# A three-block fp32 transformer kernel on one core: the first block's mixer run in two passes, tokens 0 to 127 first, with expert rows gathered beside the second pass

## The chip, the cores and the metric

The kernel runs on one core of one Trainium2 chip. The metric is device time in microseconds (us) of one execution; lower is better. A core has five engines, each with its own instruction stream: TensorE (PE), VectorE (DVE), ScalarE (ACT), GpSimd (POOL) and SyncE (SP), which here only issues DMAs. They meet through semaphores.

## The reference, cut to what matters

Three blocks run one after the other on 512 tokens of 1024 features, all in fp32. Only the first is changed. It is a mixer (retention and spatial gating) and then a layer that picks, for each token, 128 of 16384 experts:

```python
mod = silu(c) @ w_ada + b_ada                 # six rows: shift, scale, gate, twice
h = modulate(rms_norm(x, norm1_g), shift1, scale1)
q, k, v, g_ret, u, sv, gate_a, gate_b = split(h @ w_in)        # 1024 -> 7168
y_ret = head_norm(retention(rotary(q), rotary(k), v), ret_gn_g) # causal over all 512 tokens
branch_a = (silu(g_ret) * y_ret) @ w_ret_out
branch_b = spatial_gating(gelu(u), gelu(sv), ...) @ w_sgu_out   # mixes within 128 tokens
x = x + gate1 * ((sigmoid(gate_a) * branch_a + sigmoid(gate_b) * branch_b) @ w_out)
h2 = modulate(rms_norm(x, norm2_g), shift2, scale2)
s = einsum(h2 @ w_q, sub_keys)                # 8 heads, two halves, 128 keys each
expert, g = top 16 of the 16 x 16 sums of the two halves' top 16, softmax   # 128 picks a token
act = gelu(einsum('td,thkd->thk', h2, expert_u[expert])) * g
x = x + gate2 * einsum('thk,thkd->td', act, expert_v[expert])
```

A token needs only itself and earlier tokens of the mixer, so tokens 0 to 127 can go through the whole mixer before the others.

## The kernel before, in words

Tokens stand in 4 tiles of 128 partitions. A projection is cut into chunks of 512 output columns, a chunk into two pieces (halves of the 1024 inputs) of 1 MB. `load_ahead` (L94) has SP load the pieces into `ring_raw` in an order fixed by `plan_one` (L1924). `split_piece` (L135) has DVE make two rounded parts of each piece, `ring_high` (a cast, L130) and `ring_low` (a subtraction, L132). PE then takes three fast products in place of one plain fp32 product (`product`, L174, lines L176 to L178). A matmul of plain fp32 operands has two records in the trace, each with its weight load; one of the split parts has one.

The first block (`block_one`, L1917) is a row of stages with a barrier between them:

- `first_rows` (L929) is the entry: the first two of the six `mod` rows are summed on DVE from eight 1 MB lines of `w_ada` (`add_lines`, L920, recorded as L923), the input is normed, transposed on PE and split into `h_features`.
- `first_mixer` (L1339) runs 20 chunks for all 4 tiles, in ten calls of `project`, `project_along` and `closing`. The last 16 lines of `w_ada` are added beside the first chunks. Rotary, retention, norms and gating are interleaved with the projections by hand-made tables (L1064 to L1066). `closing` (L720) adds to `x`, norms each tile and transposes it (L770).
- `peer` (L1492) computes the queries of all tokens (16 query blocks, pieces of `peer_w_q`), scores them against the keys (`score_unit`, L1580), and `route` has DVE find the top 16 and the expert numbers. One unit is 2 heads, 32 picks of each of 128 tokens; a tile has 4 units. For pick n of a tile POOL gathers one row per token (L1566): 128 rows of 8 KB, u and v side by side, 1 MB. DVE takes the product of u with `h` (`dot`, L1756) and PE adds the v half into PSUM with two plain fp32 matmuls by a scaled diagonal (L1655), which DVE makes (`weigh`, L1749). There are 4 x 128 = 512 picks. The first 10 are gathered during the query stage and summed on DVE instead (`sum_early`, L1769); the rest follow at the speed of the gathers, through 12 slots of SBUF.
- `leave` (L1427) closes the block.

What sets the order around the change: each engine's stream is in program order; SP issues a piece when its slot is free; POOL gathers into a slot when its former pick has been used (`used_slot` or `taken_early`).

Of the kernel before, what the change touches and what calls it, by code (L numbers as in the profile page):

```python
# [23 lines left out]
P = 128  # L24
SEQ = 512
NT = SEQ // P
D = 1024
# [50 lines left out]
def over(nc, under, name, shape, dtype=F32):  # L78

    return nc.alloc_sbuf_tensor_at(f"{name}_{next(NUMBERS)}", shape, dtype, offset=PLACES[under.name])  # L80
# [828 lines left out]
SGU_GROUPS, SGU_DIM = 4, 256  # L909

# [14 lines left out]

WARMING = 4


def first_rows(nc, core, d, mod, c_col, gain):  # L929
# [5 lines left out]
    plan_splits(core, 1)  # L935
    with stage(nc, "entry", "zeroed", "c_loaded", "bias_loaded", "gain_loaded", "silu_done", "used", "multiplied", "summed", "shift_ready",
# [6 lines left out]
        def _(sp):  # L943
# [6 lines left out]
            load_ahead(core, sp, core.splits + 2)  # L950
# [12 lines left out]
        def _(act):  # L963
# [14 lines left out]
            copy_transposed(nc, core, act, KD, core.hT[0], transposed, copied)  # L978
# [16 lines left out]
        def _(dve):  # L995
# [9 lines left out]
            def lower(t):  # L1005
                for n in (2 * t, 2 * t + 1):
                    at = transposed_bank(KD, n)
                    dve.wait_ge(copied, n + 1)
                    nc.vector.tensor_tensor(core.hT[1][at], transposed_view(core, n), core.hT[0][at].bitcast(F32), ALU.subtract)
# [12 lines left out]
            split_piece(nc, core, dve, 0, 0)  # L1022
# [7 lines left out]
            for t in range(NT):  # L1030
# [4 lines left out]
                if t == 2:  # L1035
                    lower(0)
# [3 lines left out]


def other_rows(nc, core, d, mod, c_col):

    ring = over(nc, core.h, "ada_ring", [P, 2, ADA_LINE])
    lines = [(part, k) for k in range(KD) for part in (1, 2)]
    signals = ("ada_used", "ada_landed0", "ada_landed1")

    def pool_part(pool, used, *landed):
        for n, (part, k) in enumerate(lines):
            if n >= 2:  # L1050
                pool.wait_ge(used, n - 1)
            pool.dma_start(ring[:, n % 2, :], ada_lines(d, part, k)).then_inc(landed[n % 2], 16)

    def dve_part(dve, used, *landed):
        for n, (part, k) in enumerate(lines):
            dve.wait_ge(landed[n % 2], 16 * (n // 2 + 1))
            rows = mod[:, 2 * part:2 * part + 2, :].rearrange("p a f -> p (a f)")
            add_lines(nc, dve, rows, ring[:, n % 2, :], c_col[:, k:k + 1]).then_inc(used, 1)
            yield

    return signals, pool_part, dve_part, None, None


# [5 lines left out]
def retention(nc, core, d, mod, qk, v, rot, qkT, y, cosine, sine):  # L1069
# [13 lines left out]
    def pe_part(pe, loaded, rotated, transposed, moved, spread, cleared, decay_loaded, scored, weighted, summed, copied):  # L1083
        def spread_rows(n):
            for q in (2 * n, 2 * n + 1):
                if q >= 4:
                    pe.wait_ge(cleared, q - 3)
                nc.tensor.matmul(core.ps[:, q % 4, :], core.ones[:], rows[:, q * BANK:(q + 1) * BANK], start=True, stop=True).then_inc(spread, 1)

        def turn(t):  # L1090
            pe.wait_ge(rotated, t + 1)
            if t:
                pe.wait_ge(moved, 2 * t)
# [3102 lines left out]
```

## Time and profile before

| | us |
|---|---|
| median of 3 runs | 4110.15 (4108.12 to 4110.21) |
| the profiled execution, its span from first to last instruction | 4104.9 |
| entry | 0 to 55.9 |
| mixer of the first block, all 4 tiles | 55.9 to 583.9 |
| query stage, with 20 gathers issued | 583.9 to 690 |
| gathering stage of the first block | 690 to about 1956 |
| second and third block | the rest |

No time of the profiled execution other than its span is given; the median of the runs is 5.25 us above that span, for what lies around it. Over the span PE is busy 87%, DVE 69%, POOL 22%, ACT 20%. In the page's slices the DMA engines are busy 9 tenths or more from about 720 to 1950 us, and 2 to 6 tenths in the mixer. Busy shares of PE there are of modelled ends: a record lasts longer than the distance to the next one, so the pace of PE is read from the distance between starts.

### The profile page before, as it was taken

To read this page: it belongs to the slowest core of one execution; us is meant where nothing else is said; L and a number is where in the kernel's file an instruction comes from. 1 tells how busy PE (TensorE), PEld (TensorE's weight loads), DVE (VectorE), ACT (ScalarE), POOL (GpSimd) and SP (SyncE) were. 2 spreads that over 40 slices of the span, in tenths; PEclk is the share of its full clock that TensorE was granted. 3 is DMA by queue.
4 is the path that set the end of the run, shared out by engine and by line. 5 is a ranking of instruction groups with operands and counts; after the bars stand their busy time and mean duration, and the time that the engine had idled before them with its cause. 6 is when DMAs were issued, how large, how long until landed. Compare 5 with 4: busy or idle time off the path is not lost. (4 is left out here: it accounts for less than half of the span.)

```text
span 4104.9 us, 43525 instructions
## 1 busy us (share of the span) xinstructions
PE 3577.6 (87%) x15786; PEld 2429.3 (59%) x15786; DVE 2847.4 (69%) x5103; ACT 836.9 (20%) x1657; POOL 903.5 (22%) x852
## 2 busy tenths in 40 slices
PE   7999988878778777777899997967978999999998
PEld 5778876223223222222667776856756787877876
DVE  7653668878878877865755567666867558757775
ACT  1110112111111111110121135316842212411000
POOL 2010003434444444443000111214630000100000
PEclk9999999999999999999999998988988999999999
DMA  6522227999999999998334522119953233222221
GB/s 252 176 83 93 96 103 302 419 423 423 423 423 424 423 420 416 412 418 357 119 120 136 171 83 102 58 65 399 421 226 93 65 106 97 84 95 94 99 87 70
DMA packets 206417, 910.60 MB, mean 222 GB/s; under 512 B 20830, under 2 KB 25838, under 8 KB 126738
## 3 DMA queue, kind: packets, MB, share of 16 engines
q0 software_dynamic: 93040, 665.54, 39.7%
q1 hardware_dynamic: 108272, 233.47, 17.0%
q10 hardware_dynamic: 4900, 8.94, 0.6%
q8 instruction: 119, 1.95, 0.2%
q14 instruction: 86, 0.70, 0.0%
HBM read 878.97 MB, written 40.97 MB: 224 GB/s over the span
## 5 line engine op out<-in xcount | busy, mean ns | idle before, releaser
L130 DVE CAST ring_high<-ring_raw 128x2048 fp32r<-128x2048 f32 (+2 forms) x166 | 192.4, 1159 | 426.9 <-PE psum L178 348.1
L176 PE MATMUL psum<-ring_high,h_features 128*128 128x512 f32 x1128 | 459.3, 407 | 23.9 <-PEq L48 16.0
L178 PE MATMUL psum<-ring_high,h_features 128*128 128x512 f32 x1128 | 446.3, 396 | 0.0
L177 PE MATMUL psum<-ring_low,h_features 128*128 128x512 f32 x1128 | 445.8, 395 | 0.0
L1655 PE MATMUL psum<-slots_ring,evacuation_tmp 128*128 128x512 f32 x672 | 334.2, 620 | 92.6 <-DVE evacuation_tmp L1749 92.6
L132 DVE TENSOR_TENSOR ring_low<-ring_raw,ring_high 128x2048 fp32r<-128x2048 f32 (+2 forms) x166 | 358.1, 2157 | 12.8 <-issue 0.4
L176 PE MATMUL psum<-h_features,ring_high 128*128 128x512 f32 (+3 forms) x888 | 350.7, 395 | 14.0 <-DVEq L287 5.5
L177 PE MATMUL psum<-h_features,ring_high 128*128 128x512 f32 (+3 forms) x888 | 347.2, 391 | 0.0
L178 PE MATMUL psum<-h_features,ring_low 128*128 128x512 f32 (+3 forms) x888 | 346.7, 390 | 0.0
L1871 ACT ACTIVATE weight<-score 128x1 f32<-128x1 f32 x512 | 103.6, 203 | 1124.8 <-DVE score L1756 1124.6
L1655 PE MATMUL psum<-slots_features,evacuation_tmp 128*128 128x512 f32 x504 | 250.1, 620 | 64.3 <-DVE evacuation_tmp L1749 64.2
L1655 PEld LDWEIGHTS psum<-slots_ring,evacuation_tmp 128*128 128x128 f32 x672 | 114.7, 190 | 311.3 <-DVE evacuation_tmp L1749 227.9
L176 PEld LDWEIGHTS psum<-ring_high,h_features 128*128 128x128 f32 x1128 | 216.5, 192 | 73.7 <-issue 15.9
L1756 DVE CUSTOM_DVE_ANT_0 slots_ring<-slots_ring,h_tokens 128x1024 f32<-128x1024 f32 x168 | 205.5, 1223 | 76.4 <-DMA slots_ring<-in_peer_uv,expert 73.5
L178 PEld LDWEIGHTS psum<-ring_high,h_features 128*128 128x128 f32 x1128 | 215.5, 191 | 47.1
L177 PEld LDWEIGHTS psum<-ring_low,h_features 128*128 128x128 f32 x1128 | 216.6, 192 | 42.5 <-issue 0.5
L1566 POOL DMA_INDIRECT slots_ring<-in_peer_uv,expert x168 | 175.9, 1047 | 252.0 <-PE psum L1655 235.1
L1655 PEld LDWEIGHTS psum<-slots_features,evacuation_tmp 128*128 128x128 f32 x504 | 86.4, 190 | 227.2 <-DVE evacuation_tmp L1749 164.5
L645 POOL TENSOR_SCALAR mean_var<-mean_var 128x1 f32<-128x1 f32 (+3 forms) x25 | 11.3, 452 | 941.8 <-DVEq L3961 378.1
L1655 PE MATMUL psum<-slots_raw,evacuation_tmp 128*128 128x512 f32 x332 | 165.7, 622 | 46.9 <-DVE evacuation_tmp L1749 46.9
L1655 PE MATMUL psum<-slots_mod,evacuation_tmp 128*128 128x512 f32 x336 | 165.7, 617 | 41.5 <-DVE evacuation_tmp L1749 41.4
L176 PEld LDWEIGHTS psum<-h_features,ring_high 128*128 128x128 f32 (+2 forms) x888 | 166.0, 187 | 53.7 <-issue 10.1
(667 smaller groups left out, 7003.9 us busy)
## 6 DMA issues: line engine op xcount, KB each, us to landing
ring_raw<-in_w_in SPq DMA_DIRECT2D x94, 1024.0 KB, 5.3
ring_raw<-in_w_up_pairs SPq DMA_DIRECT2D x20, 1024.0 KB, 5.0
ada_ring<-in_w_ada POOLq DMA_DIRECT2D x16, 1024.0 KB, 5.5
ring_raw<-in_w_out SPq DMA_DIRECT2D x12, 1024.0 KB, 5.0
moe_entries<-in_const_zero_rows POOLq DMA_DIRECT2D x23, 512.0 KB, 5.0
row_room<-moe_entries SPq DMA_DIRECT2D x23, 512.0 KB, 11.0
moe_results<-rows_out SPq DMA_DIRECT2D x23, 512.0 KB, 7.6
ring_raw<-in_w_down SPq DMA_DIRECT2D x10, 1024.0 KB, 4.8
```

Of the source, the lines that this page charges most:

```text
L130: nc.vector.tensor_copy(high, whole)
L132: return nc.vector.tensor_tensor(low, whole, high.bitcast(F32), ALU.subtract)
L176: nc.tensor.matmul(out, a[0], b[0], start=start, stop=False)
L177: nc.tensor.matmul(out, a[0], b[1], start=False, stop=False)
L178: return nc.tensor.matmul(out, a[1], b[0], start=False, stop=stop)
L645: nc.gpsimd.tensor_scalar(v, v, eps, None, ALU.add).then_inc(done, 1)
L1566: nc.gpsimd.indirect_dma_start(out=slots[slot_of[n]], out_offset=None, in_=rows, in_offset=bass.IndirectOffsetOnAxis(ap=expert[:, t, i:i + ...
L1655: mm = nc.tensor.matmul(banks(t)[q], diagonal[:, n % DIAGONALS, :], slots[slot_of[n]][:, D + q * BANK:D + (q + 1) * BANK], start=i == (0 i ...
L1756: nc.vector.tensor_tensor_reduce(out=u, in0=u, in1=core.h[:, t, :], scale=1.0, scalar=0.0, op0=ALU.mult, op1=ALU.add, accum_out=score[:, i ...
L1871: nc.scalar.activation(weight[:, i:i + 1], score[:, i:i + 1], ACT.Gelu).then_inc(activated, 1)
```

## The change

The mixer of the first block becomes one stage that runs 20 chunks twice. The first pass takes tile 0 alone, with plain fp32 matmuls whose moving operand is the piece as loaded, so nothing is split (`mixer_pe`, the branch `p.native`). It ends with the four query chunks, the scores and the routing of tile 0. The second pass takes tiles 1 to 3 with split pieces, loaded again; the cast is now ACT's and the subtraction DVE's. Beside it, DVE routes units 1 to 3 of tile 0 and takes the dot products of 57 picks, ACT scales their v rows (`scale_picks`), and POOL adds them up (`add_pick`), through 5 slots. The query stage then holds only tiles 1 to 3, with 20 more picks taken the same way, and the gathers that are left (the PE sum starts at pick 77) go through 13 slots. Retention in the second pass takes tile 0's keys and values from what the first pass kept.

```diff
-EARLY = 10
-SLOTS_UV = 12
+EARLY_PICKS = 57
+POOL_PICKS = 77
+SLOTS_UV = 13
...
+ALONE_SLOTS = [n % WIDE_SLOTS for n in range(40)] + [4, 5, 0, 2, 6, 7, 1, 3]
...
+def mixer_pe(nc, core, pe, p):
+    for q, (c, half) in enumerate(p.pieces[0:2 * MIX_CHUNKS]):
+        for i in range(n):
+            pace.until(due(p.at["pe"], n * q + i))
...
+                if p.native:
+                    mm = nc.tensor.matmul(bank(c, i), x[0], w[0], start=kk == 0, stop=kk == KD - 1)
+                else:
+                    mm = product(nc, bank(c, i), x, w, kk == 0, kk == KD - 1)
...
+def scale_picks(nc, act, k, lo, hi):
+    act.wait_ge(k.dotted, hi)
+    nc.scalar.activation(k.weight[:, lo:hi], k.score[:, lo:hi], ACT.Gelu).then_inc(k.activated, hi - lo)
...
+        nc.scalar.activation(v, v, ACT.Copy, scale=k.weight[:, n:n + 1]).then_inc(k.scaled, 1)
...
+def add_pick(nc, core, pool, k, n):
...
+        pool.wait_ge(k.taken, n)
+        nc.gpsimd.tensor_tensor(total, total, v, ALU.add).then_inc(k.taken, 1)
...
+        one = Pass(sems[0:len(PASS_SIGNALS)], (0,), True, ALONE_PIECES)
+        two = Pass(sems[len(PASS_SIGNALS):2 * len(PASS_SIGNALS)], (1, 2, 3), False, REST_PIECES)
...
+            mixer_pe(nc, core, pe, one)
+            for j in range(UNITS):
+                query(j)
+                if j:
+                    score_unit(j - 1)
+            mixer_pe(nc, core, pe, two)
...
+            for n in range(EARLY_PICKS):
+                q = due(REST_DOTS, n)
+                pace.until(due(two.at["pool"], q + 1))
+                add_pick(nc, core, pool, k, n)
+                gather_until(n)
```

Where side work stands is set by tables of step numbers; two lines of them, each number the piece (for PE the piece and tile) before which a step is taken:

```diff
+           "dve": [4, 4, 5, 8, 9, 10, 11, 12, 13, 13, 14, 14, 15, 15, 23, 24, 24, 24, 25, 26, 28, 28, 29, 30, 31, 31, 35, 35, 35, 36, 36, 36],
+REST_ROUTE = [7, 15, 23, 26, 26, 28, 35, 42, 47, 52, 57, 62, 62, 62, 65, 69, 76, 78]
```

On PE, the mixer began with three split products for each quarter of a piece (before):

```order
L176 MATMUL psum<-ring_high,h_features 128x512
L177 MATMUL psum<-ring_low,h_features 128x512
L178 MATMUL psum<-ring_high,h_features 128x512
L176 MATMUL psum<-ring_high,h_features 128x512
L177 MATMUL psum<-ring_low,h_features 128x512
```

The same place after, from the last chunk of the first pass over the start of the queries (`wide_` are pieces as loaded, `alone_cT` and `h_alone` are tile 0's features):

```order
L1038 MATMUL psum<-wide_80,alone_cT_337 128x512 x4
L1038 MATMUL psum<-wide_81,alone_cT_337 128x512 x4
L1062 MATMUL psum<-ident,h_tokens 128x128 x8
L1938 MATMUL psum<-h_alone_77,wide_82 128x128 x4
L1938 MATMUL psum<-h_alone_77,wide_83 128x128 x4
```

A piece of the first pass is 4 matmuls where it was 48, and the 8 transposes of the closed tile stand directly between the last chunk and the queries.

On DVE, where the retained heads are normed, before (`gate_a` stage):

```order
L627 BN_STATS bn_parts<-a 128x6 x16
L630 BN_AGGR mean_var<-bn_parts 128x2 x16
L1249 SCALAR_TENSOR_TENSOR mod<-mod,row_b 128x1024
L1254 TENSOR_SCALAR a<-a,mean_var 128x256 x4
L1257 TENSOR_TENSOR a<-a,x_tokens 128x1024
L130 CAST ring_high<-ring_raw 128x2048
L132 TENSOR_TENSOR ring_low<-ring_raw,ring_high 128x2048
```

The same place in the second pass (L1703 is the dot product of a pick, L1226 the subtraction for one piece):

```order
L1226 TENSOR_TENSOR rest_raw_low_340<-wide_79,ring_high 128x2048
L1342 TENSOR_SCALAR a<-a,mean_var 128x256 x4
L1345 TENSOR_TENSOR a<-a,x_tokens 128x1024
L1342 TENSOR_SCALAR a<-a,mean_var 128x256 x4
L1345 TENSOR_TENSOR a<-a,x_tokens 128x1024
L1703 ISA slots_first_75,score<-slots_first_75,h_tokens 128x1024
L1703 ISA score 128x1
L1226 TENSOR_TENSOR ring_low<-wide_82,ring_low 128x2048
L1703 ISA slots_mod_74,score<-slots_mod_74,h_tokens 128x1024
L1703 ISA score 128x1
```

The casts have left DVE, and dot products and routing steps now stand between the splits.

On POOL, the mixer before held DMA issues and a few small operations; in the second pass it reads so (`fifth`, `slots_first` and `slots_mod` are slots of gathered rows, `x_tokens` the running sum):

```order
L1731 TENSOR_TENSOR x_tokens<-x_tokens,fifth 128x1024
L1692 DMA fifth<-in_peer_uv,expert 128x2048
L1731 TENSOR_TENSOR x_tokens<-x_tokens,slots_first_75 128x1024
L1692 DMA slots_first_75<-in_peer_uv,expert 128x2048
L1731 TENSOR_TENSOR x_tokens<-x_tokens,slots_mod_74 128x1024
L1692 DMA slots_mod_74<-in_peer_uv,expert 128x2048
```

Each gather stands behind the addition that frees its slot; there are 76 such additions of 128 x 1024 and one copy.

## Rows read from the trace of the kernel before

**Rows 1.** Busy time of each engine by stretch: mixer, query stage, gathering stage.
```profile
core 0: us, PE busy (x) PEld busy (x) DVE busy (x) ACT busy (x) POOL busy (x), PEclk, DMA share, GB/s
55.90:583.90 528.00, 505.12 (x2240) 410.07 (x2240) 304.53 (x323) 70.24 (x116) 34.79 (x35) 0.98 0.35 121
586.00:690.00 104.00, 98.33 (x476) 84.18 (x476) 74.46 (x174) 33.04 (x48) 27.72 (x21) 0.97 0.61 226
690.00:1936.00 1246.00, 985.22 (x2039) 344.69 (x2040) 986.70 (x2444) 143.40 (x545) 529.45 (x505) 0.99 1.01 419
```

**Rows 2.** Timeline, POOL then PE, gathering stage: start us, us, engine, line, operation.
```profile
689.92 1.07 POOL L1566 DMA_INDIRECT slots_mod<-in_peer_uv,expert  x1 [0.30 <-issue]
...
899.51 0.98 POOL L1566 DMA_INDIRECT slots_rows<-in_peer_uv,expert  x1 [1.51 <-PE psum L1655]
...
1952.04 3.70 PE L1655 MATMUL psum<-slots_mod,evacuation_tmp 128*128 128x512 f32 x8 [0.44 <-DVE evacuation_tmp L1749]
```

**Rows 3.** Timeline of PE: split products, score matmuls; weight loads of plain fp32.
```profile
71.22 0.39 PE L177 MATMUL psum<-ring_low,h_features 128*128 128x512 f32 x1
71.45 0.39 PE L178 MATMUL psum<-ring_high,h_features 128*128 128x512 f32 x1
...
597.01 1.05 PE L1580 MATMUL psum<-keysT,qT 128*128 128x128 f32 x8
598.95 0.33 PE L176 MATMUL psum<-h_features,ring_high 128*128 128x384 f32 x1
599.12 0.33 PE L177 MATMUL psum<-h_features,ring_high 128*128 128x384 f32 x1
...
22.74 0.19 PEld L986 LDWEIGHTS psum<-x_tokens,ones 128*128 128x128 f32 x1 [0.24 <-issue]
```

**Rows 4.** Groups by line and shape, DVE: from 0 to 700 us; last, gathering stage.
```profile
L132 DVE TENSOR_TENSOR ring_low<-ring_raw,ring_high 128x2048 fp32r<-128x2048 f32 x40 | 91.7, 2292 | 3.3 <-issue 0.4
L923 DVE SCALAR_TENSOR_TENSOR mod<-ada_ring,c_col,mod 128x2048 f32<-128x2048 f32 x23 | 54.1, 2352 | 25.6 <-DMA ada_ring<-in_w_ada 15.7 <-DMA mod<-in_b_ada 8.8
L130 DVE CAST ring_high<-ring_raw 128x2048 fp32r<-128x2048 f32 x40 | 49.0, 1225 | 141.7 <-PE psum L178 121.7 <-PEq L48 20.0
L1756 DVE CUSTOM_DVE_ANT_0 slots_mod<-slots_mod,h_tokens 128x1024 f32<-128x1024 f32 x6 | 7.2, 1222 | 3.1 <-DMA slots_mod<-in_peer_uv,expert 3.1
...
L1749 DVE TENSOR_SCALAR evacuation_tmp<-ident,weight,gates 128x128 f32<-128x128 f32 x494 | 169.4, 343 | 0.0
```

**Rows 5.** DVE and POOL at once: a group, then timelines of 246 and 2549 us.
```profile
L1238 POOL TENSOR_TENSOR x_tokens<-x_tokens,row_a 128x1024 f32<-128x1024 f32 x2 | 4.8, 2392 | 64.7 <-DMA row_b<-in_norm_g 64.7
...
246.01 5.52 DVE L1254 TENSOR_SCALAR a<-a,mean_var 128x256 f32<-128x256 f32 x4 [3.19 <-POOL mean_var L647]
256.25 1.38 DVE L1254 TENSOR_SCALAR a<-a,mean_var 128x256 f32<-128x256 f32 x4
...
2548.67 2.27 DVE L165 TENSOR_TENSOR ring_low<-ring_raw,ring_high 128x2048 fp32r<-128x2048 f32 x1
2550.86 1.28 DVE L2529 TENSOR_TENSOR keys<-hgrn_drop,k 128x256 f32<-128x256 f32 x1
2552.07 0.41 DVE L2530 TENSOR_TENSOR queries<-hgrn_drop,q 128x256 f32<-128x256 f32 x1
...
2548.84 3.02 POOL L2495 TENSOR_TENSOR hgrn_drop<-logs 128x512 f32<-128x512 f32 x1
```

**Rows 6.** Group by line and shape, ACT, the entry's scaled copy.
```profile
L974 ACT ACTIVATE h_tokens<-x_tokens,mean_var 128x1024 f32<-128x1024 f32 x4 | 4.6, 1148 | 22.3 <-POOL mean_var L960 22.3
```

**Rows 7.** Timeline of PE where the mixer closes: the last tiles' transposes.
```profile
571.27 1.04 PE L770 MATMUL psum<-ident,h_tokens 128*128 128x128 f32 x8
581.92 1.97 PE L770 MATMUL psum<-ident,h_tokens 128*128 128x128 f32 x8 [6.10 <-DVE h_tokens L860]
```

**Rows 8.** Timeline of the query stage: the first gather on POOL, its dot on DVE.
```profile
623.28 1.12 POOL L1566 DMA_INDIRECT slots_mod<-in_peer_uv,expert  x1 [35.09 <-DVE expert L1732]
...
629.00 1.23 DVE L1756 CUSTOM_DVE_ANT_0 slots_mod<-slots_mod,h_tokens 128x1024 f32<-128x1024 f32 x1 [1.12 <-DMA slots_mod<-in_peer_uv,expert]
```

More of the change, by code:

```diff
@@ L10 @@
 from contextlib import ExitStack, contextmanager
-from itertools import count
+from itertools import chain, count
 import numpy as np
@@ L1039, in _ @@
             lower(3)
[L1042 to L1061, printed above, removed]
@@ new lines, with raise_scores, start_gather @@
+TO_SHIFTED, ROUTE_STEPS = 17, 26
+def raise_scores(nc, act, k, m):
+    t, j = divmod(m, UNITS)
+    top = k.gates[:, t % 2, UNIT_HEADS * j:UNIT_HEADS * (j + 1), :]
+    act.wait_ge(k.shifted, m + 1)
+    nc.scalar.activation(top, top, ACT.Exp).then_inc(k.raised, 1)
+def start_gather(nc, pool, k, rows, n):
+    t, i = divmod(n, PICKS)
+    nc.gpsimd.indirect_dma_start(
+        out=k.slots[k.slot_of[n]], out_offset=None, in_=rows,
+        in_offset=bass.IndirectOffsetOnAxis(ap=k.expert[:, t, i:i + 1], axis=0),
+    ).then_inc(k.arrived[k.slot_of[n]], 16)
@@ new lines, in gather @@
+                def gather(n):
+                    slot, before = k.slot_of[n], k.last_of[n]
+                    if n % Q == 0:
+                        pool.wait_ge(k.routed, n // Q + 1)
+                    if before is None:
+                        if slot in (5, 6):
+                            pool.wait_ge(core.split[slot - 5], first + UNITS)
+                        elif slot in (7, 8):
+                            pool.wait_ge(core.used, first + UNITS)
+                        else:
+                            pool.wait_ge(projected, 1)
+                    elif before < POOL_PICKS:
+                        pool.wait_ge(k.taken, before + 1)
+                    else:
+                        pool.wait_ge(used_slot, before - POOL_PICKS + 1)
+                    start_gather(nc, pool, k, rows, n)
@@ L1570, in _ @@
+                for n in range(EARLY_PICKS, POOL_PICKS):
+                    add_pick(nc, core, pool, k, n)
+                    while k.issued < POOL_PICKS + 5 and k.last_of[k.issued] is not None and k.last_of[k.issued] <= n:
+                        gather(k.issued)
+                        k.issued += 1
+                for n in range(k.issued, TOTAL_PICKS):
+                    t, i = divmod(n, PICKS)
+                    gather(n)
                     if t and i == ROOT_PICKS[0]:
@@ L1843, in _ @@
                         weigh(n - 1)
-                    advance(router, 2 if n < EARLY + 6 else 1)
+                    advance(router, 1)
+                    if n % Q == Q - 1:
+                        for _ in router:
+                            pass
                     if t and i == 4:
@@ L1943 @@
+def plan_one(d):
+    return [("peer_q", cut) for cut in query_chunks(d)]
 STRIP = [0, 512, 896, 1152]
```

1554 lines of the change are left out of this document (968 added, 586 removed).

## The prediction

> **What bounds the kernel now.** I read the stages first: the windows by stretch [rows 1] cut the first block into mixer (528.0 us), query stage (583.9 to 690, 106 us) and gathering (1246 us of it). In the mixer PE is busy 505.1 of 528.0, DVE 304.5, and the DMA engines 35%: PE sets the pace and memory is idle. In the gathering stage the DMA share is 1.01 at 419 GB/s, and PE and DVE are at 79% each: the gathers set the pace. The timeline of that stage [rows 2] agrees: POOL's issues are 0.98 + 1.51 = 2.49 us apart and each waits for PE to release a slot that DMA filled. One pick is 1.049 MB, which at 419 GB/s is 2.50 us. So 128 rows gathered beside the mixer are worth 2.50 us each, if mixer work hides them.
>
> **Gathers, the gain.** At 690 us 20 gathers have been issued (POOL's 21 instructions in that window less one iota [rows 1]); the last matmuls end at 1952.04 + 3.70 = 1955.7 us [rows 2], 492 picks later. After the change POOL issues pick n when pick n-5 has been added, up to pick 81, and the eight new slots at once: 90 are out when the query stage ends. 70 fewer remain: 70 x 2.50 = **-175 us**. This is the whole gain; everything else is what it costs.
>
> **Mixer, PE's own work.** Split products of 512 columns start 0.2267 us apart (71.22 and 71.45, rounded), those of 384 columns 0.174 [rows 3]. A weight load of a plain fp32 matmul of 512 columns takes 0.19 after an idle 0.24, two loads to a matmul: 0.43 a record and 0.858 a matmul. Eight records of 128 columns take 1.05 with a tail of about 0.28: 0.11 a record, 0.22 for a score matmul [rows 3]; 0.43 and 0.64 for 256 and 384 columns follow by length.
> - Before: 1920 x 0.2267 = 435.3; 20 sets of 8 transposes x 0.88 = 17.6; retention scores 8.6, their products 17.2, spatial mixing 6.9, spreading `mod` 6.9: 492.5. The stage took 528.0, so 35.5 went in waits and in stretches at the lower clock.
> - First pass: 160 x 0.858 = 137.3, where this tile's share was 108.8; 5 sets of transposes, one tile's retention and mixing, the spreading 15.6: 152.9. Queries 128 x 0.22 = 28.2 and 16 score matmuls 3.5: 31.7.
> - Second pass: 1440 x 0.2267 = 326.4; transposes 13.2, scores 7.7, products 36 x 0.43 = 15.5, mixing 5.2: 368.0.
>
> Sum 552.6, which is 60.1 more than before.
>
> **Mixer, what is lost around it.** Memory in the first pass: 34 pieces, 13 `w_ada` lines and some 3.5 MB of constants, about 53 MB, at 419 GB/s [rows 1] 126 us against 153 of PE, with six pieces ahead. It is covered; if that cover went, each missing us would be PE's. With one tile there is no other tile's work over a chain, so I take 12 for waits inside the pass (bounds 0 and 35). Its close is bare: evacuation, statistics, two small POOL steps, gain, shift, transpose, copy. The mixer's last tile before shows PE waiting 6.10 for such a chain, and its 8 transposes then taking 1.97 instead of 1.04 [rows 7]; before they start and until the queries follow I take 12 (bounds 6 and 20). Start of the second pass, whose first splits are behind 12 routing steps on DVE: 5. Its own close over three tiles, two last splits and the barrier: 13.
>
> **DVE in the second pass.** Before, its mixer time was 304.5 [rows 1]: less 16 lines x 2.352 and 40 pieces x (1.225 + 2.292) [rows 4] leaves 126.2 for four tiles, 94.7 for three. Now: 40 subtractions 91.7, tiles 94.7, 57 dot products x 1.30 (1.22 and the reading of the sum) = 74.1, and 4 routed units. A unit: DVE was busy 986.7 in the gathering stage [rows 1]; 492 picks at 1.30 + 0.34 less what overlaps, taken as 1.50 [rows 4], and some 45 for the tiles' closings leave about 204 for 14 units, 14.6 each. Sum 319 busy, some 331 with the gaps between dependent instructions. Of it 8 lies under the queries and 33 behind PE's last product: 290 beside PE's 368. By itself DVE would be covered.
>
> But DVE and POOL get in each other's way. POOL's addition of 128 x 1024 takes 2.39 us. At 246 us, beside POOL's other two such operations (L1241), four DVE instructions took 5.52 where the next four took 1.38. At 2548.67 DVE subtracts in 2.27; POOL's 128 x 512 sum, started 0.17 later, takes 3.02 and ends at 2551.86, and DVE's next multiplication, begun at 2550.86, takes 1.28 where its twin takes 0.41 [rows 5]. Each waits for the other. The change puts 57 additions, 137 us of POOL, beside a DVE whose splits and dot products read two operands from SBUF. An addition costs DVE nothing when it has other work, and 2.39 at most. I take 1.6: in both pictures DVE loses most of POOL's time, and a third of its work is searches with one operand. 57 x 1.6 = 91, DVE 381 against PE's 368. Two nearly equal engines in program order wait on each other; I add 13 for the excess and 12 for that: 25 (bounds 0 and 71). ACT gets 42 casts, 57 scalings of 1.15 us [rows 6] and the old evacuations, under 260 us in all: no bound, nothing charged.
>
> The Trainium skill, "SBUF — State Buffer", section "Who interferes with whom", says that a DVE instruction with two SBUF inputs and a GpSimd instruction that reads SBUF exclude each other wholly. The trace agrees in direction. Losses 12 + 12 + 5 + 25 + 13 = 67; the mixer stage takes 619.6 instead of 528.0: **+91.6**.
>
> **Query stage.** Before 106 with PE busy 98. Now PE has 384 x 0.174 = 66.8 and 3.5 for scores. DVE has 6 subtractions and part of a cast, 15, 20 dots 26, one unit 20 with gaps, and 20 additions of POOL 32: 93, of which a few can lag into the gathering. POOL itself: 20 x (2.39 + 1.3) = 74. I take 90 with the barrier: **-16**. Bounds 75 and 112.
>
> **Entry.** One split of 3.5 leaves DVE, partly hidden behind a PE wait: **-3**.
>
> Sum: -175 + 91.6 - 16 - 3 = -102.4. The sum is made against the profiled span of 4104.9, the median is 5.25 above and I leave that distance alone: 4110.15 - 102.4 = **4008 us**. A measurement of this kernel tells 0.2%, 8 us, from no change.
>
> **Rivals.**
> - *The overlap is as good as before.* The mixer loses only its former 35.5 (+60.1), the query stage takes 78 (-28). 4110.15 - 175 + 60.1 - 28 - 3 = 3964 us. For it: DVE's load per piece is uneven, and three pieces of lookahead smooth it. Against: rows 5. Chance 17%.
> - *POOL's additions exclude DVE wholly.* DVE has 290 + 57 x 2.39 = 426, and with 13 for order 439: 46 more than the 393 I took. The query stage gets 20 x 0.8 = 16 more and about 3 of order. 4008 + 65 = 4073 us. For it: in rows 5 DVE's second operation waits for POOL to its end. Against: a third of DVE's work does not contend there. Chance 16%. The page named above would make this outcome of its rule, if every addition met such an instruction.
> - *The first pass starves PE, and it runs at 1.2 GHz: slower than before.* With one tile every chain (rotary, scores, norm, gating) faces its own projections; after a 6.10 us wait the transposes took twice as long [rows 7]. At the lower level the 184.6 us of PE in pass and queries double: +185 less 15 of chains hidden then, 4178 us. It decides above 102/185 = 55% of that work at 1.2 GHz. Against: a piece is 3.43 us of unbroken matmuls, and the granted clock was 0.98 over the old mixer [rows 1]. Chance 8%.
> - *The 57 picks do not stay out of the way.* A pick goes through gather, dot, scaling, addition; if the five slots turn too slowly, the backlog is waited for in the query stage and the gain is given back: 41 late picks x 2.50 cancel it, near 4110. Against: the first gather was issued at 623.28 and its dot began at 629.00, 5.7 later [rows 8]; with 1.3, 1.6 and 2.4 for dot, scaling and addition that makes 11 to 12 us, over five slots 2.4 a pick, and the pass has 6.5. Chance 4%.
>
> **Numbers.** Forecast 55%. The range from 3955 to 4085 takes in the first three cases with the bounds of the losses, and leaves out the slow one and some of the tails. Faster by over 0.2%: 87%; within: 4%; slower: 9%.
>
> **What would show it.** The gathers' pace unchanged at 2.49 and 90 issued when the query blocks end. First pass: plain matmuls 0.86 apart, 165 us; queries start about 230, the second pass about 265 and ends about 660. POOL additions above 2.4 us and DVE's dots above 1.22 when they meet. Wrong would be: gathers of the last stage further apart, a granted clock under 0.9 from 60 to 250 us, or a second pass over 450 us.

## The result and the profile after

The change made the kernel slower: 4126.99 us (4124.03 to 4132.23, 4 runs) against 4110.18 for the kernel before in the same set of runs, a ratio of 1.0046 with a 95% interval of 1.0032 to 1.006. I had forecast 4008. The profiled execution has a span of 4122.3 us, 17.4 more than before.

Windows of the kernel after: first pass, queries, second pass, query stage up to the 90th gather's issue, the rest of the gathering stage. They answer to [rows 1].

```profile
core 0: us, PE busy (x) PEld busy (x) DVE busy (x) ACT busy (x) POOL busy (x), PEclk, DMA share, GB/s
54.00:227.50 173.50, 159.28 (x401) 74.51 (x401) 67.17 (x67) 23.84 (x40) 9.10 (x9) 0.96 0.94 351
227.50:265.00 37.50, 37.50 (x301) 36.99 (x302) 16.77 (x62) 9.11 (x11) 0.00 (x0) 0.93 0.39 133
265.00:741.20 476.20, 392.49 (x1678) 314.57 (x1676) 394.57 (x537) 242.79 (x322) 270.93 (x137) 0.91 0.66 235
741.20:876.20 135.00, 84.78 (x424) 80.58 (x425) 87.86 (x127) 49.66 (x82) 86.76 (x48) 0.78 0.66 235
876.20:1964.50 1088.30, 862.74 (x1797) 304.69 (x1795) 843.74 (x2051) 121.81 (x471) 444.81 (x435) 0.99 0.99 414
```

The timeline, POOL at the end of the query stage (its 83rd and 90th gathers), then PE's last product of a pick; they answer to [rows 2].

```profile
866.41 1.12 POOL L1692 DMA_INDIRECT slots_raw<-in_peer_uv,expert  x1 [0.30 <-issue]
...
876.18 1.10 POOL L1692 DMA_INDIRECT slots_features<-in_peer_uv,expert  x1 [0.30 <-issue]
...
1962.59 1.88 PE L2293 MATMUL psum<-slots_raw,evacuation_tmp 128*128 128x512 f32 x4
```

The gain is there. Before, 492 gathers were left at 690 us and the last products ended at 1955.7, 2.573 us a pick. Now 422 are left at 876.2, and the end at 1964.5 is 1088.3 later, 2.579 a pick: the stage is 178 us shorter (1265.7 - 1088.3 = 177.4). But it starts 186.2 us later. Both passes of the mixer run to 741.2 instead of 583.9, and the query stage takes 135.0 instead of 106. The last products come 8.8 us later than before, and what follows them takes 2157.8 us instead of 2149.2 with the same instructions: that makes the 17.4.

**The first pass** went as forecast: queries from 227.5, second pass from 265, at a granted clock of 0.96 and 0.93. Its close reads on PE's timeline, and answers to [rows 7]:

```profile
224.76 1.97 PE L1062 MATMUL psum<-ident,h_tokens 128*128 128x128 f32 x8 [6.52 <-DVE h_tokens L1270]
```

**The second pass** is what went wrong: 476 us, where 411 were forecast. PE is busy for 392 of it and idle for 84, and DVE is busy for 395, 83%. Groups of DVE and POOL in the pass (the subtractions in two rows by buffer, the dot products and the additions by one of their three buffers); they answer to [rows 4, 5]:

```profile
L1226 DVE TENSOR_TENSOR rest_raw_low<-wide,ring_high 128x2048 fp32r<-128x2048 f32 x26 | 65.4, 2515 | 47.6 <-ACT ring_high L1984 47.6
L1226 DVE TENSOR_TENSOR ring_low<-wide,ring_low 128x2048 fp32r<-128x2048 f32 x13 | 38.2, 2936 | 10.4 <-ACT ring_low L1984 10.1
L1703 DVE CUSTOM_DVE_ANT_0 slots_mod<-slots_mod,h_tokens 128x1024 f32<-128x1024 f32 x30 | 61.2, 2053 | 0.0
L1731 POOL TENSOR_TENSOR x_tokens<-x_tokens,slots_mod 128x1024 f32<-128x1024 f32 x29 | 73.1, 2520 | 40.5 <-ACT slots_mod L1719 40.1
```

A subtraction alone takes 2.29 and a dot product 1.22. Here the means are 2.52 to 2.94 and 2.05. The timeline of the query stage shows why:

```profile
777.33 2.29 DVE L165 TENSOR_TENSOR ring_low<-ring_raw,ring_high 128x2048 fp32r<-128x2048 f32 x1 [4.90 <-ACT ring_high L158]
779.04 2.83 POOL L1731 TENSOR_TENSOR x_tokens<-x_tokens,slots_mod 128x1024 f32<-128x1024 f32 x1 [8.05 <-ACT slots_mod L1719]
779.54 3.42 DVE L1703 CUSTOM_DVE_ANT_0 fifth<-fifth,h_tokens 128x1024 f32<-128x1024 f32 x1
782.89 1.21 DVE L1703 CUSTOM_DVE_ANT_0 slots_first<-slots_first,h_tokens 128x1024 f32<-128x1024 f32 x1
783.81 2.49 POOL L1731 TENSOR_TENSOR x_tokens<-x_tokens,slots_mod 128x1024 f32<-128x1024 f32 x1
784.03 3.35 DVE L1703 CUSTOM_DVE_ANT_0 slots_mod<-slots_mod,h_tokens 128x1024 f32<-128x1024 f32 x1
787.49 0.20 ACT L1710 ACTIVATE weight<-score 128x3 f32<-128x3 f32 x1 [7.49 <-DVE score L1703]
```

A dot product that starts while an addition runs takes 3.4 us, 2.2 more, and ends 1.1 us after the addition; one that has started first (at 782.89, the addition at 783.81) takes 1.21. At the end ACT has stood 7.49 us before the three scores, with the evacuation that PE's next block needs behind it.

I had three theories. **A:** POOL's additions and the picks' own work load DVE until it sets the pace. **B:** ACT stands in program order between DVE's scores and PE's casts and evacuations, and the order costs the time. **C:** the gathers crowd the transfers of the weights.

### The profile page after: what moved, and what is told of

Its sections match the earlier page's. It is cut to its first block and busy times, and to the rows that moved or that the text cites. A ratio compares the mean times of both kernels' runs of the same rounds, so it can differ in the third digit from the quotient of the medians.

```text
span 4122.3 us, 43270 instructions
## 1 busy us (share of the span) xinstructions
PE 3510.3 (85%) x15594; PEld 2397.7 (58%) x15594; DVE 2874.9 (70%) x4977; ACT 1036.0 (25%) x1866; POOL 1116.3 (27%) x920
## 5 line engine op out<-in xcount | busy, mean ns | idle before, releaser
L130 DVE CAST ring_high<-ring_raw 128x2048 fp32r<-128x2048 f32 (+3 forms) x126 | 143.2, 1137 | 285.2 <-PE psum L178 235.0
L176 PE MATMUL psum<-ring_high,h_features 128*128 128x512 f32 x672 | 275.5, 410 | 15.4 <-PEq L48 11.0
L132 DVE TENSOR_TENSOR ring_low<-ring_raw,ring_high 128x2048 fp32r<-128x2048 f32 (+3 forms) x126 | 266.4, 2114 | 9.4
L178 PE MATMUL psum<-ring_high,h_features 128*128 128x512 f32 x672 | 266.2, 396 | 0.0
L177 PE MATMUL psum<-ring_low,h_features 128*128 128x512 f32 x672 | 266.0, 396 | 0.0
L1703 DVE CUSTOM_DVE_ANT_0 slots_mod<-slots_mod,h_tokens 128x1024 f32<-128x1024 f32 x144 | 212.1, 1478 | 49.1 <-DMA slots_mod<-in_peer_uv,expert 47.6
L1692 POOL DMA_INDIRECT slots_mod<-in_peer_uv,expert x144 | 174.4, 1211 | 195.4 <-PE psum L2293 134.7
L176 PEld LDWEIGHTS psum<-h_features,ring_high 128*128 128x128 f32 (+3 forms) x760 | 142.2, 187 | 47.7 <-issue 9.5
L2293 PE MATMUL psum<-slots_low,evacuation_tmp 128*128 128x512 f32 x264 | 132.5, 625 | 39.9 <-DVE evacuation_tmp L2309 39.8
L178 PEld LDWEIGHTS psum<-h_features,ring_low 128*128 128x128 f32 (+3 forms) x760 | 142.2, 187 | 33.8 <-issue 1.8
L177 PEld LDWEIGHTS psum<-h_features,ring_high 128*128 128x128 f32 (+3 forms) x760 | 142.3, 187 | 32.7 <-issue 1.9
L176 PEld LDWEIGHTS psum<-ring_high,h_features 128*128 128x128 f32 x672 | 129.3, 192 | 45.1 <-issue 9.3
```

The source lines that it names most:

```text
L130: nc.vector.tensor_copy(high, whole)
L132: return nc.vector.tensor_tensor(low, whole, high.bitcast(F32), ALU.subtract)
L176: nc.tensor.matmul(out, a[0], b[0], start=start, stop=False)
L177: nc.tensor.matmul(out, a[0], b[1], start=False, stop=False)
L178: return nc.tensor.matmul(out, a[1], b[0], start=False, stop=stop)
L1692: nc.gpsimd.indirect_dma_start(out=k.slots[k.slot_of[n]], out_offset=None, in_=rows, in_offset=bass.IndirectOffsetOnAxis(ap=k.expert[:, t, ...
```

## The experiments

The thin_ runs, rows32 and no_gelu leave out part of the picks' work and so give other sums than the reference; all other runs leave out nothing. Marks in each profile: the second pass ends where SP issues the query stage's first load (265.0 is taken as its start in all of them); the "query part" runs from there to the first gather into a new slot; the last product of a pick; and the rest of the span.

| run | second pass | its DVE busy | query part | last product | rest |
|---|---|---|---|---|---|
| changed kernel | 476 | 395 | 125.2 | 1964.5 | 2157.8 |
| thin_adds | 444 | 314 | 100.7 | 1911.0 | 2158.4 |
| thin_dots | 454 | 320 | 108.9 | 1926.3 | 2153.2 |
| thin_scaling | 470 | 389 | 117.7 | 1950.2 | 2157.5 |
| thin_all | 429 | 255 | 84.1 | 1880.2 | 2156.2 |
| rows32 | 470 | 385 | 123.5 | 1957.1 | 2164.1 |
| thin_rows32 | 397 | 254 | 77.3 | 1839.5 | 2158.7 |
| no_picks_early | 396 | 245 | | 2074.1 | 2143.1 |
| casts_ahead | 475 | 388 | 125.2 | 1963.7 | 2157.7 |
| dve_adds | 472 | 381 | 102.9 | 1948.9 | 2155.7 |
| none_in_queries | 479 | 392 | 50.0 | 1953.9 | 2154.6 |
| one_to_a_piece | 426 | 324 | 49.7 | 1956.1 | 2153.4 |
| one_dve_add | 417 | 327 | 54.9 | 1951.2 | 2154.9 |

The second pass is the same code in the changed kernel, in none_in_queries and in evacuate_first, and took 476.2, 479.3 and 474.7 us: a difference of under 5 us in this column says nothing.

### One operation of a pick made thin

```diff
 thin_adds (add_pick)
-        nc.gpsimd.tensor_tensor(total, total, v, ALU.add)
+        nc.gpsimd.tensor_tensor(total[:, 0:64], total[:, 0:64], v[:, 0:64], ALU.add)
 thin_dots (dot_pick): u[:, 0:64] and core.h[:, t, 0:64] for n < POOL_PICKS
 thin_scaling (scale_picks): v is slot[:, D:D + 64]
```

> POOL's 76 additions of picks to the first tile's rows (L1731) cover 64 columns instead of 1024, so the first 128 tokens' sums and all that follows from them are left incomplete; gathers, dot products, scalings and all waits stay. Reference in the changed kernel: second pass 265 to 741 (476 us), first new slot's gather in the query stage issued at 866 (125 us after 741), last pick's products end at 1964.5, span 4122.3. Theory A (POOL's additions hold DVE up: its dot products took 1.21 or 3.4 us, its subtractions 2.29 or 2.8 to 4.0): second pass 400 to 420 us, query part 90 to 100, last pick near 1870. Theory B (ACT stands in program order between DVE's dot products and PE's casts and evacuations, whatever POOL does): second pass 450 to 476, query part 110 to 125. Theory C (the gathers crowd the weights' transfers): no change of either, or worse, since gathers then come sooner.

> DVE's dot products of the first 77 picks (L1703) cover 64 columns instead of 1024, so these picks' scores are not the reference's; the rest stays. It takes 57 x 2.05 = 117 us of busy DVE out of the second pass, and some 40 out of the query part. Theory A: the subtractions still meet POOL's additions, but DVE is far from its bound: second pass 410 to 430. Theory B: the score is there sooner when ACT asks for it, second pass 420 to 440. Theory C: no change. If the pass stays above 450, DVE's load was not the bound.

> ACT's scaling of the first 77 picks' rows (L1719) covers 64 columns instead of 1024, so these picks' sums are not the reference's; the additions stay whole. It takes 57 x 1.15 = 66 us of ACT out of the second pass and 1.1 us out of the lap of every slot. Theory A: second pass 465 to 476. Theory B: ACT reaches casts and evacuations sooner: 430 to 455. Theory C: no change.

One run each: 4071.11, 4081.2 and 4109.42 us, beside 4107.91 for the kernel before. The second pass fell by 32, 22 and 6 us, the query part by 24.5, 16.3 and 7.5. DVE's groups in thin_adds:

```profile
L1226 DVE TENSOR_TENSOR rest_raw_low<-wide,ring_high 128x2048 fp32r<-128x2048 f32 x26 | 59.5, 2289 | 71.9 <-ACT ring_high L1984 71.5 <-issue 0.2
L1226 DVE TENSOR_TENSOR ring_low<-wide,ring_low 128x2048 fp32r<-128x2048 f32 x13 | 29.9, 2303 | 23.8 <-ACT ring_low L1984 23.7
L1703 DVE CUSTOM_DVE_ANT_0 slots_mod<-slots_mod,h_tokens 128x1024 f32<-128x1024 f32 x30 | 37.5, 1263 | 3.1 <-DMA slots_mod<-in_peer_uv,expert 3.1
```

The durations are back at 2.29 and 1.26. DVE's busy time in the pass fell from 394.6 to 314.0 us: the 56 additions had held it up for 80.6 us, 1.44 each. Theory A holds in kind, but not alone: thin_adds' pass of 444 missed the 400 to 420 that A gave. thin_dots missed as well: A gave 410 to 430, and I had written that above 450 DVE's load would not be the bound. It was 454, with DVE busy for 320. So something besides DVE's load holds the pass, and taking that load away shows only part of what it costs.

### The passes without picks, and all three operations thin

```diff
 no_picks_early
-EARLY_PICKS = 57
-POOL_PICKS = 77
+EARLY_PICKS = 1
+POOL_PICKS = 1
+REST_TAKEN = [(0, 0)] * 39 + [(0, 1)]
 thin_all: the three edits above together
```

> Both passes stay, but of the first tile's picks only one is taken in the second pass and none in the query stage; PE takes the other 511 in the gathering stage (nothing is left out; the gathering stage starts with 18 picks over three slots and is long). This measures the second pass and the query stage with no picks beside them. Picks are the whole excess: second pass 390 to 405 us (368 of PE and some 25 of losses), query part 78 to 90. The pass is slow by itself (three tiles in turn over a DVE and an ACT that are asked for other work too): 430 or more, the 444 that were left in thin_adds.

> Dot products, scalings and additions of the first 77 picks all cover 64 columns (their sums are not the reference's); gathers, waits, table loads and the order of every queue stay. Engine time is the excess: second pass within 10 us of no_picks_early. Queue coupling and transfers are: 15 to 40 us above it, since ACT still waits for scores behind gathers that have to land, and gathers still share the DMA engines with the weights. Query part 85 to 100.

no_picks_early: 4218.94 us in one run, since PE takes nearly all picks in the gathering stage; what it is for is the pass, 396 us. So the passes by themselves cost what the sum said, and the picks cost 80. The pass cut at the 15th, 21st and 39th subtraction, the kernel after and then no_picks_early:

```profile
core 0: us, PE busy (x) PEld busy (x) DVE busy (x) ACT busy (x) POOL busy (x), PEclk, DMA share, GB/s
265.00:419.10 154.10, 143.59 (x642) 117.60 (x641) 123.46 (x269) 72.90 (x87) 45.84 (x24) 0.98 0.51 180
419.10:496.30 77.20, 55.16 (x223) 43.48 (x222) 61.16 (x80) 43.12 (x58) 45.11 (x24) 0.82 0.63 232
496.30:695.90 199.60, 169.91 (x727) 135.14 (x726) 168.33 (x146) 113.27 (x159) 154.59 (x74) 0.94 0.82 295
695.90:741.20 45.30, 23.83 (x91) 18.36 (x90) 41.62 (x45) 13.50 (x20) 25.39 (x17) 0.73 0.47 162
```

```profile
265.00:410.70 145.70, 140.76 (x638) 115.98 (x637) 103.20 (x252) 49.22 (x56) 16.67 (x9) 1.00 0.39 133
410.70:463.40 52.70, 50.83 (x222) 41.07 (x221) 33.62 (x58) 17.77 (x16) 0.00 (x0) 0.97 0.36 120
463.40:623.10 159.70, 159.70 (x724) 131.60 (x723) 79.90 (x79) 54.16 (x51) 2.82 (x6) 1.00 0.42 139
623.10:660.90 37.80, 22.44 (x99) 17.70 (x98) 28.57 (x39) 9.44 (x12) 7.33 (x8) 0.80 0.24 83
```

The excess is 8, 24.5, 40 and 7.5 us. In the third stretch, 18 pieces with 33 picks, PE could go at 8.87 us a piece (159.7 / 18, PE busy throughout). DVE now has 9.35 us of work a piece (168.3 / 18), more than PE, and the spacing is 11.1. By its work DVE is over PE there, though over the whole pass the two are equal. The second stretch has 24.5 us in six pieces: there the last routing stands on DVE together with picks, and ACT waits behind both (the routing alone is in no_picks_early too). Three lines of ACT and DVE in the kernel after:

```profile
443.20 0.23 ACT L1686 ACTIVATE gates<-gates 128x32 f32<-128x32 f32 x1 [11.27 <-DVE gates L1662]
448.75 1.88 ACT L1984 CAST ring_high<-wide 128x2048 fp32r<-128x2048 f32 x1
450.67 2.79 DVE L1226 TENSOR_TENSOR rest_raw_low<-wide,ring_high 128x2048 fp32r<-128x2048 f32 x1 [7.51 <-ACT ring_high L1984]
```

thin_all: 4038.1 us in one run, pass 429. With DVE at 255 busy, 33 us of the 80 are left, which DVE's work does not explain.

### What holds the other 33: order, bytes or table loads

```diff
 casts_ahead (ACT's part in mixer: all of a piece's picks behind the next cast)
-                if q and REST_TAKEN[q - 1][1]:
-                    scale_picks(nc, act, k, REST_DOTS[q - 1] - REST_TAKEN[q - 1][1], REST_DOTS[q - 1])
+                if q and sum(REST_TAKEN[q - 1]):
+                    scale_picks(nc, act, k, REST_DOTS[q - 1] - sum(REST_TAKEN[q - 1]), REST_DOTS[q - 1])
 rows32: slot[0:32], expert[0:32] in the gather, and [0:32] in the operations on it, for n < POOL_PICKS
 no_gelu: ACT.Gelu -> ACT.Copy in scale_picks
 thin_casts_ahead, thin_rows32, thin_no_gelu: the same edits on top of thin_all
```

> In the second pass ACT scales all of a piece's picks behind the next cast, not one of them ahead of it; nothing is left out. Theory B (casts wait on ACT behind scores, 99 us of such waits in the pass): second pass 445 to 465, total 4095 to 4115. If the waits only move to other instructions of ACT (evacuations), 470 to 480 and 4120 to 4130.

> The first 77 picks are gathered, multiplied, scaled and added for 32 of the 128 tokens only (the other 96 tokens miss them); every instruction, wait and order stays, and an operation on 32 partitions should take as long as on 128. Only the bytes fall, to a quarter. Reference: 265 to 741 (476 us) in the changed kernel, 396 with no picks. In the pieces that take two picks, three transfers of 1.05 MB go into some 9 us. Theory C (the gathers crowd the weights, which land late, and ACT's casts waited 38 us for them): second pass 445 to 460. Without C: 470 to 478.

> The first 77 picks' weights are taken without the Gelu (a copy in its place, so their sums are not the reference's), which takes the picks' 13 function table loads in the second pass away and most of the 12 that bring the other functions back: up to 20 x 1.28 = 26 us of ACT. If ACT is a bound there: second pass 455 to 468. If not: 472 to 478.

Beside the full work none of them gave much: passes of 475, 470 and 476 us, totals of 4123.16 (ratio 1.0042, 1.0029 to 1.0055), 4122.78 and 4126.62. For casts_ahead the waits only moved. The wait rows of ACT and DVE, kernel after and then casts_ahead (total, times, longest):

```profile
ACT weight L1710 <- DVE score L1703: 99.3, 25, 8.9
DVE rest_raw_low L1226 <- ACT ring_high L1984: 47.6, 14, 7.5
```

```profile
ACT weight L1710 <- DVE score L1703: 84.5, 17, 11.9
DVE rest_raw_low L1226 <- ACT ring_high L1984: 31.0, 9, 6.0
```

DVE could have covered a gain, so each was tried again in thin_all:

> thin_all (dot products, scalings and additions of the first 77 picks over 64 columns, their sums not the reference's) with the scalings behind the next cast, as in casts_ahead. thin_all: second pass 429 us. If a cast behind a score on ACT holds the 33 us: 400 to 415. If not: 425 to 430.

> thin_all with the gathers (and the thin operations) for 32 of the 128 tokens, as in rows32; the sums are not the reference's. If the gathers' bytes make the weights and the picks land late: second pass 400 to 415 instead of 429. If not: 425 to 430.

> thin_all without the picks' Gelu, as in no_gelu, so 20 function table loads fewer in the second pass; the sums are not the reference's. If the loads delay ACT's evacuations and casts: second pass 405 to 420 instead of 429. If not: 427 to 430.

Passes of 431, 397 and 419 us (totals, one run each, 4042.49, 3999.89 and 4027.85). **The gathers' transfers are the 33 us**: with a quarter of their rows and bytes (the edit cuts both together), and every instruction, wait and table load still there, the pass is that of no_picks_early within 1 us. Two windows, thin_all and thin_rows32:

```profile
265.00:693.80 428.80, 386.29 (x1674) 312.77 (x1673) 255.41 (x536) 197.47 (x322) 136.14 (x137) 0.95 0.71 261
```

```profile
265.00:661.60 396.60, 374.35 (x1675) 305.76 (x1673) 254.16 (x536) 197.17 (x322) 131.99 (x137) 0.97 0.53 159
```

The rows of DMA issues show it for the weights: ten pieces of `w_in`, and as the last number the median time in us from issue to landing, in no_picks_early between 463 and 623 us, then in thin_all between 470 and 656.

```profile
wide<-in_w_in SPq DMA_DIRECT2D x10, 1024.0 KB, 5.1
```

```profile
wide<-in_w_in SPq DMA_DIRECT2D x10, 1024.0 KB, 8.2
```

In the kernel after it is 6.9; thin_rows32's rows give no landing time. Memory is not full over the pass (share 0.71; 0.85 from 475.7 to 656.8 us, where most picks stand), yet a piece that shares the DMA engines with picks of the same size lands 3 us later, and the second pass holds only three pieces. So there are two excesses, and each hides most of the other: the picks' work on the engines alone makes 74 (rows32), their transfers alone 33 (thin_all), both together 80. Theory C, which rows32 alone had seemed to exclude by the mark that I had set (470 to 478 without C), is true of the 33; theory B fell. The table loads' 10 us in thin_no_gelu lie inside the 33 and are gone when DVE is loaded.

### Where the picks stand

```diff
 one_to_a_piece (on casts_ahead and none_in_queries)
+EARLY_PICKS = POOL_PICKS = 35
+REST_TAKEN = [(0, 0)] * 3 + [(0, 1), (0, 0)] + [(0, 1)] * 7 + [(0, 0)] + [(0, 1)] * 27
 after_the_chains (on one_to_a_piece; NARROW_PICKS is the number of picks that go through three slots before five are in use)
-NARROW_PICKS = 18
+NARROW_PICKS = 5
+REST_TAKEN = [(0, 0)] * 19 + [(1, 1)] * 17 + [(0, 1)] + [(0, 0)] * 3
```

> both_orders with 35 instead of 57 picks in the second pass, at most one to a piece of weights. Nothing is left out. In the changed kernel the first 14 pieces (at most one pick each) ran 8 us behind the pass with no picks, the 25 behind them (two each) 64 us. If the excess belongs to two picks a piece: second pass 405 to 425, query stage starts at 670 to 690, the 22 picks more cost 55 us later, total 4085 to 4110. If each pick costs the same (80 / 57 = 1.4 us): second pass 445, total 4125 to 4135.

> one_to_a_piece with the same 35 picks in other places: none beside the first 19 pieces (rotary, retention, routing), two to a piece from the 20th to the 36th. Nothing is left out. one_to_a_piece had its second pass in 426 us, 30 above no picks: 9 of it by piece 18, 21 behind. If a pick costs where it meets DVE's chains: 405 to 418. If each pick costs the same wherever it stands: 422 to 430. If two to a piece is what costs (1.9 us a pick in the changed kernel's last 25 pieces): 440 to 460.

one_to_a_piece: 4112.18 us (ratio 1.0013, 1.0002 to 1.0024), pass 426. after_the_chains: 4121.74 (1.0039, 1.0025 to 1.0053), pass 443, with DVE busy for 170 of the 207 us of its fullest 18 pieces. The same 35 picks cost 30 us one to a piece and 47 two to a piece, all of the 47 in those 18 pieces: it is the load of a piece that counts, not the chains, though one_to_a_piece's total was just behind the bound that I had given (4085 to 4110).

### The query stage

```diff
 none_in_queries
-POOL_PICKS = 77
+POOL_PICKS = 57
-HEAD_TAKEN = (2, 2, 3, 2, 3, 3, 3, 2)
+HEAD_TAKEN = (0,) * 8
 evacuate_first (ACT): head_picks(2 * j) behind the four evacuations and the casts instead of ahead
 both_orders: casts_ahead and none_in_queries
```

> In the query stage ACT evacuates a block's four banks and casts the next pieces before it waits for the picks' dot products, not behind it; nothing is left out. Theory B: PE no longer waits for the picks' lap: the new slots' gathers are issued 15 to 25 us sooner (845 instead of 866), total 4102 to 4112. Theory A: POOL's additions and DVE set the pace of the stage, and the issue stays at 860 to 866, total within 5 us of 4127.

> The 57 picks stay in the second pass; the query stage takes none (POOL_PICKS 57), PE takes the 20 in the gathering stage at 2.49 us each, 50 us. Nothing is left out. Second pass unchanged at 474 to 478. If the 20 picks cost the stage more than their 50 us, the total falls: query part 75 to 85 instead of 125, total within 8 us of 4127 either way, 4119 to 4135. Had my sum been right (the stage 90 with the picks, 78 without), the total would rise by 38.

> casts_ahead and none_in_queries together: the 57 picks in the second pass, none in the query stage. Nothing is left out. If both gains add: total 4109 less what casts_ahead gains against the changed kernel, 4085 to 4110.

evacuate_first: 4122.29 us (ratio 1.0035, 1.0024 to 1.0046), the new slots 3.6 us sooner: the order on ACT is a small part. none_in_queries: 4109.14 us (1.001, 1.0001 to 1.002), which undoes most of the loss, and more of it than I had expected (4119 to 4135). Its query part and the stretch to its last product:

```profile
744.30:794.30 50.00, 49.94 (x284) 49.97 (x285) 11.67 (x6) 14.35 (x16) 0.00 (x0) 0.96 0.50 169
794.30:1953.90 1159.60, 925.18 (x2018) 342.88 (x2016) 898.42 (x2191) 136.01 (x510) 472.37 (x462) 0.99 0.98 409
```

PE is now busy without a gap. The 20 picks had lengthened this part by 75 us and shortened the gathering by 61.5 (1159.6 - 1098.1, where 1098.1 is the changed kernel's stretch from its first gather into a new slot to its last product). The table divides the 75: with thin operations the part is 84.1, 41 us less; with a quarter of the gathered rows as well it is 77.3, 7 less. The 27 that are left belong to the picks' round of waits and orders by elimination only; evacuate_first is the one run that changed an order there. both_orders: 4110.94 (1.0015, 1.0005 to 1.0025), nothing more, as casts_ahead gains nothing.

### DVE adds instead of POOL

```diff
 dve_adds (add_pick, on DVE one piece behind the dot product; ACT's scaling of the row is gone)
-        nc.gpsimd.tensor_tensor(total, total, v, ALU.add)
+        nc.vector.scalar_tensor_tensor(total, v, weight, total, ALU.mult, ALU.add)
 both also: POOL gathers at most 3 picks ahead of the second pass's 57 (35), not 5; evacuations first on ACT, as in evacuate_first
 dve_adds: POOL_PICKS = 73, HEAD_TAKEN = (2,) * 8, so 16 picks in the query stage, not 20
 one_dve_add: the same with one_to_a_piece's table and no picks in the query stage
```

> POOL's addition and ACT's scaling become one DVE operation per pick, x = v * weight + x (128x1024, about 1.3 us), one piece behind the dot product; POOL only gathers; 16 instead of 20 picks in the query stage, whose evacuations come first on ACT. Nothing is left out. Theory A (an addition on POOL costs DVE up to 2.2 us of exclusion and the slot 2.4 us more): DVE does less in all, second pass 410 to 440, query part 95 to 105, total 4040 to 4075. Theory B: DVE is the bound and gets 74 us more work of its own, so the pass stays at 465 to 480 and the total at 4100 to 4127.

> one_to_a_piece with DVE's multiply-and-add in place of ACT's scaling and POOL's addition: 35 picks at most one to a piece, none in the query stage. Nothing is left out. DVE's busy time should fall from 323 to some 245 + 35 x 2.5 = 333, so if DVE's busy time alone decides, second pass 425 to 430 and total 4110; if being stopped by POOL is worse than work of its own, 410 to 420 and 4092 to 4105, under the kernel before (4106.7 in this set of runs).

dve_adds: 4105.36 us (ratio 0.9997, 0.9984 to 1.001). The operation takes 1.28 us, less than POOL's addition had taken from DVE (1.44), but the pass is still 472: DVE is nearly as busy as before (380.7 for 394.6). So of the two expectations the second came true, that DVE is the bound and gets work of its own in place of being held up. The query part is 102.9 for 125.2, but with 16 picks instead of 20 and with the evacuations first, so that gain is not the addition's alone.

This run also answers a rival that I had not named, POOL: in the third stretch of the changed kernel it is busy for 154.6 of 199.6 us. The windows of the second pass, dve_adds and then thin_dots:

```profile
265.00:736.90 471.90, 391.24 (x1674) 315.22 (x1673) 380.67 (x593) 178.69 (x265) 122.97 (x78) 0.91 0.64 232
```

```profile
265.00:718.90 453.90, 390.99 (x1675) 315.46 (x1673) 320.17 (x536) 243.47 (x322) 258.68 (x137) 0.93 0.68 246
```

dve_adds takes 148 us of work from POOL, 64 from ACT and 14 from DVE, and the pass is 4 us shorter. thin_dots takes 12 from POOL, none from ACT and 74 from DVE, and the pass is 22 shorter. thin_scaling took 45 from ACT and gained 6. So among the engines it is DVE's load that holds the pass.

one_dve_add: 4108.17 (1.0004, 0.9994 to 1.0014; I had given 4092 to 4105 or 4110), pass 417, 9 less than one_to_a_piece, though DVE is no less busy (327 for 324). ACT's scaling is gone in it too, so the 9 cannot be put down to POOL's additions alone. Both versions beat the changed kernel; neither can be told from the kernel before. No run that leaves nothing out is clearly faster than the kernel before.

## Why the prediction was wrong

- **Gathers, the gain: right.** -175 forecast, -177.4 between the marks, at an unchanged pace.
- **Entry and first pass: right.** -3 forecast, -1.9 measured; queries at 227.5 (230 forecast), second pass from 265, as said. Memory was nearer to the edge than "covered": DMA share 0.94 over the pass. The rival that the first pass starves PE did not come.
- **Second pass, PE's own work and the losses around it: right within 10 us.** Without picks it takes 396; my terms without the 25 gave 386 (368 + 5 + 13).
- **"DVE in the second pass" failed, in the step from 381 against 368 to 25 us.** The inputs were sound: DVE lost 1.44 us to an addition where I took 1.6, and was busy 395 in all where my terms made 410, or 422 with the gaps. But I compared totals of the whole pass. Picks are not spread evenly: in the 18 pieces that hold 33 of them DVE has 9.35 us of work a piece against PE's 8.87, and early pieces give nothing back. The 12 for program order was too small as well: DVE was busy for 84% of that stretch and waited for ACT's casts in the rest, and the spacing was 11.1. Measured: 80, where 25 was charged and 71 was my upper bound.
- **What was missing: memory in the second pass.** I had read "memory is idle" from the old mixer's 35% and counted DMA bytes for the first pass alone. The changed pass has a share of 0.66, and 0.82 in its third stretch. Two picks and a piece are 3.15 MB (3 x 1.049) in 8.87 us, 355 GB/s by themselves, close to the 419 of a full stream. It costs 33 us where DVE does not hide it.
- **Query stage failed: 90 forecast, 135 measured.** I took DVE's 93, POOL's 74 and PE's 67 as if they ran side by side. The picks go round through DVE, ACT and POOL in turn, five slots deep, and PE's evacuations stand in ACT's queue among them; without picks PE is busy for all of the stage's first 50 us. That the picks cost the stage 75 us is shown; how much of it the round makes is not.
- **The rivals.** "Exclude DVE wholly" (4073) had the mechanism: an addition met by a dot product costs it 2.2 us. Yet on average it was 1.44, not 2.39. What made the kernel slower is none of the rivals: it is the picks beside the second pass, by DVE's load in the loaded pieces and by their transfers, 55 us over the sum, and the query stage, 45 over. The last rival reckoned with five slots, but the first 18 picks go through three and only the later ones through five (`NARROW_PICKS`); no run shows the slots as the limit of the pass. My marks for wrong did name "a second pass over 450 us". The Trainium skill, "SBUF — State Buffer", section "Who interferes with whom", states that a DVE instruction with two SBUF inputs and a GpSimd instruction that reads SBUF exclude each other. Single dot products agree with it (3.35 to 3.42 us for 1.21). The mean of 1.44 is over all additions, whatever DVE did beside them; its parts were not measured.

The sum, from the forecast to the profiled span: first pass and entry +3.5, second pass without picks +10, picks beside it +55, query stage +45, gathering -2.4, the rest of the kernel +8.6, together 119.7 of the 119.8 us between 4002.5 and 4122.3.

## What to carry to other kernels

Work put beside a long stage is paid by its fullest piece, not by the stage's average: divide each engine's load, and the bytes, by the pieces that carry the extra work, and compare that with the pace of one piece. One item to a piece cost 0.9 us each here, two to a piece 1.3, and the changed kernel's 57 cost 1.4. Each saved 2.5, so beside the pass the picks still paid: 57 x 2.5 = 143 us against 80. What they left, some 62, did not cover the two passes by themselves, which without picks end 77 us later than the old mixer (660.9 for 583.9), and in the query stage 20 picks cost more than they saved (75 against 61.5). So add up the whole change before its parts are improved. When two limits lie close together, taking away one shows nothing: test each with the other already gone.

## What the hardware showed that I had not expected

- Cutting a gather and its three operations from 128 to 32 partitions left DVE's time nearly as it was (385 for 395 us busy) and took the pass from 429 to 397 once the operations were thin.
- A piece of weights took 5.1 us from issue to landing at a DMA share of 0.42, and 8.2 us where the share was 0.85.
- POOL's gather issues too are longer beside a busy DVE: their median is 1.64 us in the changed kernel's second pass and 0.94 to 0.98 in its gathering stage. The one below starts 0.9 us into a subtraction of DVE's and ends 0.8 us after it:

```profile
605.28 2.81 DVE L1226 TENSOR_TENSOR rest_raw_low<-wide,ring_high 128x2048 fp32r<-128x2048 f32 x1 [3.71 <-ACT ring_high L1984]
606.20 2.71 POOL L1692 DMA_INDIRECT slots_first<-in_peer_uv,expert  x1 [0.27 <-POOL x_tokens L1731]
```

- The rest of the kernel behind the last product, the same instructions in every version, took from 2143.1 to 2164.1 us, 2149.2 before and 2157.8 after; some 8 us of that difference comes in between 2220 and 2330 us, by ACT's timeline of both, in the next block. Its cause was not tried and stays open, and 8.6 of the 17.4 us that the change lost on the profiled span fall there. Each of these numbers is of one execution; the kernel before alone took from 4099.38 to 4116.86 us in 13 runs of one set, so part of the spread may be no more than that.
